# Hybrid attention and expert block on one core: three projections by feature tile, one gate slab moved into the last attention steps, statistics by quarters, and products of ones in three waits

## What is computed

```
h = layer_norm(concat(meta, x))
z = h @ w_in + b_in          # qa ka va | qb kb vb | forget gate | ga gb
oa = sliding_window_attention(qa, ka, va, sinks, rel_table)
ob = forgetting_attention(qb, kb, vb, cumsum(log_sigmoid(f)))
merged = sigmoid(ga) * (oa @ w_pa) + sigmoid(gb) * (ob @ w_pb)
h = layer_norm(ALPHA * h + merged @ w_o)
y = peer_ffn(h, ...)         # product keys, top 16, one-neuron experts
out = layer_norm(ALPHA * h + y)[16:]
```

## Time and profile before

| | |
|---|---|
| median of 3 executions | 1705.8 us (1704.66 to 1707.39) |
| the profiled execution's own time | 1718.5 us |
| its span | 1716.4 us |
| busy: PE, DVE, ACT, POOL | 1653.8, 1339.5, 735.2, 452.1 us |
| mean share of the DMA engines' rate | 255 GB/s |

### The profile page before, as it was taken

How to read it: one execution, slowest core, us unless ns; L and a number is a source line. 1 busy time by engine, 2 the same in 40 slices (tenths; PEclk the granted TensorE clock), 3 DMA queues, 4 the chain that set the end, 5 groups by cost and what they waited for, 6 DMA issues and landing times. The chain is left out here.

```text
span 1716.4 us, 26821 instructions
## 1 busy us (share of the span) xinstructions
PE 1653.8 (96%) x9808; PEld 1523.3 (89%) x9808; DVE 1339.5 (78%) x2848; ACT 735.2 (43%) x1288; POOL 452.1 (26%) x314
## 2 busy tenths in 40 slices
PE   5999999999979999999999999999999999999996
PEld 4897776577768899999999999999999999999996
DVE  5434554644467888999999989967989999999898
ACT  4214544333143354566766754434333333333331
POOL 0000000000001105133132432332544545457550
PEclk9999999889989999999999999999999999999998
DMA  5731111012214459699899999999999999999991
GB/s 167 198 95 55 39 48 38 25 49 86 74 61 155 129 157 379 217 341 336 269 316 340 353 307 332 341 398 392 382 400 410 407 408 408 407 402 409 407 404 78
DMA packets 185441, 438.47 MB, mean 255 GB/s; under 512 B 17832, under 2 KB 102000, under 8 KB 182880
## 3 DMA queue, kind: packets, MB, share of 16 engines
q1 hardware_dynamic: 73872, 227.43, 36.3%
q0 software_dynamic: 44080, 161.06, 25.5%
q10 hardware_dynamic: 67360, 48.28, 8.5%
HBM read 380.57 MB, written 56.13 MB: 254 GB/s over the span
## 5 line engine op out<-in xcount | busy, mean ns | idle before, releaser
L464 PE MATMUL psS<-hT_lo,hi 128*128 128x368 f32 (+2 forms) x1504 | 518.4, 345 | 4.6 <-DVE hT_lo L1021 3.9
L465 PE MATMUL psS<-hT_hi,lo 128*128 128x368 f32 (+2 forms) x1504 | 510.1, 339 | 0.0
L466 PE MATMUL psS<-hT_hi,hi 128*128 128x368 f32 (+2 forms) x1504 | 508.5, 338 | 0.0
L455 DVE TENSOR_TENSOR lo<-raw,hi 128x1024 fp32r<-128x1024 f32 x323 | 394.6, 1222 | 119.7 <-ACT hi L451 110.5
L451 ACT ACTIVATE hi<-raw 128x1024 fp32r<-128x1024 f32 x323 | 340.0, 1053 | 177.4 <-PE psS L466 124.0
L569 POOL DMA_INDIRECT gat<-in_u_rows,idx x144 | 214.7, 1491 | 393.1 <-DVE gat L1195 214.8
L464 PEld LDWEIGHTS psS<-hT_lo,hi 128*128 128x128 f32 x1504 | 283.8, 189 | 30.8 <-issue 15.6
L466 PEld LDWEIGHTS psS<-hT_hi,hi 128*128 128x128 f32 x1504 | 283.9, 189 | 13.4
L465 PEld LDWEIGHTS psS<-hT_hi,lo 128*128 128x128 f32 x1504 | 283.8, 189 | 11.1
L569 POOL DMA_INDIRECT gat<-in_v_exp,idx x144 | 220.8, 1533 | 233.9 <-DVE gat L1195 151.4
L766 ACT ACTIVATE act_hi<-act_t 128x368 fp32r<-128x368 f32 x128 | 65.6, 513 | 278.9 <-DVE act_t L1246 264.0
(11 more groups left out here) (303 smaller groups left out, 2630.1 us busy)
## 6 DMA issues: line engine op xcount, KB each, us to landing
raw<-in_u_exp SPq DMA_DIRECT2D x128, 512.0 KB
raw<-in_v_exp SPq DMA_DIRECT2D x128, 512.0 KB
gelu_dram<-gelu ACTq DMA_DIRECT2D x128, 184.0 KB
gates_dram<-gates ACTq DMA_DIRECT2D x92, 256.0 KB
gel_in<-gelu_dram SPq DMA_DIRECT2D x128, 184.0 KB
raw<-in_w_merge SPq DMA_DIRECT2D x24, 512.0 KB
gate_even<-gates_dram SPq DMA_DIRECT2D x8, 1472.0 KB
gate_odd<-gates_dram SPq DMA_DIRECT2D x8, 1472.0 KB
```

Source lines behind the costliest of these rows:

```text
L455: nc.vector.tensor_tensor(lo[:, n % RING, :], raw[:, n % RING, :], hi[:, n % RING, :].bitcast(F32), ALU.subtract).then_inc(lo_done, 1)
L464: nc.tensor.matmul(out_ap, w_h, x_l, start=start, stop=False)
L465: nc.tensor.matmul(out_ap, w_l, x_h, start=False, stop=False)
L466: return nc.tensor.matmul(out_ap, w_h, x_h, start=False, stop=stop)
```

## The change

1. Opening: DVE fills `ones` first, and PE multiplies `ones` by `ones` 52 times into bank 7; nobody reads the result. PE turns the first feature tile as soon as each token tile is normalised. DVE writes the low parts of slabs 0 to 2 ahead of all `hT_lo`. Slabs 0, 1 and 2 are then multiplied tile by tile, behind the turns of the next feature tile, into banks 4 to 7. The bias product and DVE's sum behind it (`w_done`) move behind slab 4 and slab 5.
2. Attention: `TILES` loses a tile in steps 14, 15, 32, 33, 36, 37 and two in step 38 and has 2 in each of steps 44 to 47. The 14th gate slab (v = 13) goes into bank 6 (`psO[:, 0, :]`), once the seventh block of heads is out of it. DVE's `oT_lo` comes one iteration later.
3. Merge: the gate slabs for m = 7 go ahead of all mix slabs, into both halves of `psS[:, 1]`; the weights are laid out in that order. The first slab of the output projection waits for one tile of `m_lo` at a time.
4. Statistics by quarters: two feature tiles of all token tiles share two banks (4 and 5, 6 and 7, 1 and 3, 4 and 5 again), read as four groups of 256.
5. Two more runs of products of ones, 36 behind the last turn and 30 behind the spread diagonals.

```diff
-FIRST_MIX = FIRST_MERGE + N_GATE
+FIRST_MIX = FIRST_MERGE + 2 * KT
...
-TILES = [4] * 16 + [2] * 16 + [3, 3, 2, 2, 2, 2, 2, 0] + [0] * 8
+TILES = [4] * 14 + [3] * 2 + [2] * 16 + [2, 2, 2, 2, 1, 1, 0, 0] + [0, 0, 0, 0, 2, 2, 2, 2]
...
+        def sum_bank(c, t):
+
+            return banks[((4, 5), (6, 7), (1, 3), (4, 5))[c][t // 2]]
...
+        def gate_bank(v):
+
+            return psS[:, v % 2, SEQ:] if v < N_GATE - 1 else psO[:, 0, :]
...
+            V.memset(ones[:, :], 1.0).then_inc(ones_set, 1)
...
+            for n in range(N_EARLY):
+                split_lo(dve, n)
             for k in range(KT):
                 dve.wait_ge(xT_done, k + 1)
                 dve.wait_ge(hT_hi_done, k + 1)
                 V.tensor_tensor(hT_lo[:, k, :], xT[:, k % 2, :], hT_hi[:, k, :].bitcast(F32),
                                 ALU.subtract).then_inc(hT_lo_done, 1)
-                if k < AHEAD:
-                    split_lo(dve, k)
-            V.memset(ones[:, :], 1.0).then_inc(ones_set, 1)
-
-            dve.wait_ge(bias_in, 64)
-            dve.wait_ge(w_mm, 1)
-            V.tensor_tensor(wrow[:, 0, :], psO[0:HEADS, 0, 0:3 * P], wrow[:, 1, :], ALU.add).then_inc(w_done, 1)
-            own.link(V.tensor_scalar(snk[:, 1, :], snk[:, 0, :], -1.0, None, ALU.mult))
...
-                w = block_ended(s - 3)
+                w = block_ended(s - 4)
...
-            def half_stats(c):
+            def quarter_stats(c):
 
                 dve.wait_ge(r_turned, c + 1)
                 for t in range(NBLK):
-                    ins = V.bn_stats(stats1[:, t, 6 * c:6 * c + 6], banks[4 + t])
+                    ins = V.bn_stats(stats1[:, t, 6 * c:6 * c + 6],
+                                     sum_bank(c, t)[:, t % 2 * (SEQ // 2):(t % 2 + 1) * (SEQ // 2)])
                     if t < NBLK - 1:
                         own.mark(ins)
                 ins.then_inc(r_stats_done, 1)
-                dve.wait_ge(r_stats_done, c + 1)
...
+                if m >= 3 and m % 2 == 1:
+                    quarter_stats((m - 3) // 2)
...
+            quarter_stats(3)
+            dve.wait_ge(r_stats_done, 4)
...
+            def keep_running(bank, times):
+
+                for _ in range(times):
+                    mm(bank[:, 0:P], ones[:, :], ones[:, :], start=True, stop=True)
+
             all_k = [(k, k) for k in range(KT)]
+            pe.wait_ge(ones_set, 1)
+            keep_running(banks[7], 52)
...
+            for k in range(KT + 1):
+                if k < KT:
+                    if k >= 2:
+                        pe.wait_ge(xT_done, k - 1)
+                    for t in range(NBLK):
+                        if k == 0:
+                            pe.wait_ge(norm_done, t + 2)
+                        turn(psS[:, k % 2, t * P:(t + 1) * P], xin[:, t, k * P:(k + 1) * P], ident)
+                    if k == 0:
+                        pe.wait_ge(norm_done, NBLK + 2)
+                    turn(psS[:, k % 2, SEQ:COLS], xin[0:META, NBLK, k * P:(k + 1) * P],
+                         ident[0:META, 0:META]).then_inc(turned, 1)
+                if k >= 1:
+                    j = k - 1
+                    if j == 0:
+                        pe.wait_ge(lo_done, N_EARLY)
+                    pe.wait_ge(hT_lo_done, k)
+                    for n in range(N_EARLY):
+                        halves = [slice(0, HALF), slice(HALF, COLS)] if n == 0 else [slice(0, SEQ)]
+                        for b, cols in enumerate(halves):
+                            out_ap = banks[4 + b][:, 0:HALF] if n == 0 else banks[5 + n]
+                            last = slab(n, n, out_ap, lambda k: hT_hi[:, k, cols], lambda k: hT_lo[:, k, cols],
+                                        [(j, j)], ends=(j == 0, j == KT - 1))
+                        if j == KT - 1:
+                            last.then_inc(slab_used, 1)
...
+                    mm(psO[0:HEADS, 0, 0:3 * P], relb[:, :], buck[:, :], start=True, stop=True).then_inc(w_mm, 1)
...
+                        if v == N_GATE - 1:
+                            pe.wait_ge(o_hi_done, 2 * NBLK - 1)
+                            pe.wait_ge(o_lo_done, 2 * NBLK - 1)
...
+                n = FIRST_MERGE + N_GATE + j
+                pe.wait_ge(lo_done, n + 1)
+                slab(n, n % RING, psS[:, 1, j * SEQ:(j + 1) * SEQ], tokens, tokens_lo, all_k).then_inc(slab_used, 1)
...
-                pe.wait_ge(m_lo_done, KT)
                 if m >= 2:
                     pe.wait_ge(r_done, m - 1)
-                slab(n, n % RING, psS[:, m % 2, 0:SEQ], lambda k: m_hi[:, k, :], lambda k: m_lo[:, k, :],
-                     all_k).then_inc(slab_used, 1)
+                for k in range(KT):
+                    if m == 0:
+                        pe.wait_ge(m_lo_done, k + 1)
+                    last = slab(n, n % RING, psS[:, m % 2, 0:SEQ], lambda k: m_hi[:, k, :], lambda k: m_lo[:, k, :],
+                                [(k, k)], ends=(k == 0, k == KT - 1))
+                last.then_inc(slab_used, 1)
...
+            pe.wait_ge(r_stats_done, 2)
+            keep_running(banks[7], 36)
             for part, (done, bank) in enumerate(((diag_done, 1), (shift_done, 3))):
                 pe.wait_ge(done, NBLK)
                 for t in range(NBLK):
                     last = mm(banks[bank][:, t * P:(t + 1) * P], ones[:, :], diag[:, part * NBLK + t, :],
                               start=True, stop=True)
                 last.then_inc(spread_done, 1)
+            keep_running(banks[7], 30)
```

More of the change, by code:

```diff
@@ L640, in _ @@
                                          ACT.Copy).then_inc(o_hi_done, 1)
+            for j in range(2):
+                split_hi(act, FIRST_MERGE + N_GATE + j + AHEAD)
             for m in range(KT):
@@ L644, in _ @@
                     act.wait_ge(mix_done, m - 1)
-                if m < KT - 1:
-                    split_hi(act, FIRST_MIX + m + AHEAD)
-                    for j in range(2):
+                split_hi(act, FIRST_MIX + m + AHEAD)
+                for j in range(2):
+                    if m < KT - 1:
                         nc.scalar.activation(gate[:, m % 2, j, :], gate_input(2 * m + j), ACT.Sigmoid).then_inc(gate_done, 1)
[L649 to L656, removed]
+                    else:
+                        act.wait_ge(slab_used, FIRST_MERGE + N_GATE + j + 1)
+                        nc.scalar.activation(gate[:, m % 2, j, :], psS[:, 1, j * SEQ:(j + 1) * SEQ], ACT.Sigmoid,
+                                             bias=bcol[:, N_PROJ + 8 * j + m:N_PROJ + 8 * j + m + 1]).then_inc(gate_done, 1)
                 act.wait_ge(mix_done, m + 1)
@@ L860, in halves @@
                     return v.rearrange("p (b c) -> p b c", b=2)
-                ps = halves(psS[:, n % 2, :])[:, :, 0:HALF]
+                whole = psT[:, :] if n == 0 else psS[:, n % 2, :]
+                square = banks[5 + n] if 1 <= n < N_EARLY else psS[:, n % 2, 0:SEQ]
+                ps = halves(whole)[:, :, 0:HALF]
                 if n == 0:
@@ L897, in _ @@
             dve.wait_ge(ck_in, 16)
-            for s in range(N_STEPS + 4):
+            for s in range(N_STEPS + 5):
                 last_step = 1 <= s <= N_STEPS
@@ L961, in _ @@
                                     oT_hi[:, w // NBLK, :, cols].bitcast(F32), ALU.subtract).then_inc(o_lo_done, 1)
+            for j in range(2):
+                split_lo(dve, FIRST_MERGE + N_GATE + j + AHEAD)
             for m in range(KT):
-                last = FIRST_MIX + m if m < KT - 1 else FIRST_OUT - 1
-                for n in range(FIRST_MIX + m, last + 1):
-                    split_lo(dve, n + AHEAD)
-                dve.wait_ge(slab_used, last + 1)
+                split_lo(dve, FIRST_MIX + m + AHEAD)
+                dve.wait_ge(slab_used, FIRST_MIX + m + 1)
                 dve.wait_ge(gate_done, 2 * m + 2)
@@ L1362, in _ @@
-            pe.wait_ge(bias_in, 64)
-            mm(psO[0:HEADS, 0, 0:3 * P], relb[:, :], buck[:, :], start=True, stop=True).then_inc(w_mm, 1)
+            for k in range(KT + 1):
[23 more added lines that the diff above has]
+                            last.then_inc(slab_used, 1)
@@ L1374, in _ @@
                         half = slice(b * HALF, (b + 1) * HALF)
-                        if n == 0 and b == 0:
-                            for k in range(KT):
-                                pe.wait_ge(hT_lo_done, k + 1)
-                                slab(n, 0, psS[:, 0, 0:HALF], lambda k: hT_hi[:, k, half], lambda k: hT_lo[:, k, half],
-                                     [(k, k)], ends=(k == 0, k == KT - 1))
-                            continue
                         last = slab(n, n % RING, psS[:, n % 2, b * SEQ:b * SEQ + HALF], lambda k: hT_hi[:, k, half],
```

69 lines of the change are left out of this document (32 added, 37 removed).

## The result

| | before | after |
|---|---|---|
| median | 1705.6 us (4 executions, 1704.7 to 1707.4) | 1687.3 us (4 executions, 1686.0 to 1691.1) |
| span of the profiled execution | 1716.4 us | 1686.2 us |
| busy: PE, DVE, ACT, POOL | 1653.8, 1339.5, 735.2, 452.1 us | 1659.7, 1341.2, 733.8, 449.3 us |

The ratio is 0.9895, with a 95% interval from 0.9876 to 0.9914: about 1% faster, inside the range given, but by 18.3 us and not by the 30.2 forecast. From profiled execution to profiled execution the gain is 30.2 us (1716.4 to 1686.2), so the two ways of measuring disagree by 12 us. The kernel before has two groups of execution times. Of the 69 taken in all of this study's comparisons, 44 lie between 1704.1 and 1711.2 (median 1706.7) and 25 between 1715.8 and 1724.7 (median 1717.6). The profiled execution, 1718.5, is of the upper group; the three behind the median of 1705.8 are of the lower one.

What follows compares the result with a forecast made beforehand. TensorE, working 1653.8 of 1716.4 us, was taken as the bound, with gains only in the first 510 us. The terms 3.5 + 15.5 + 6.4 + 5.8 - 1.0 = 30.2 us, off 1705.8, gave 1675.6 us; range 1667 to 1689.

Steps and rivals of the forecast that it cites:

- the median is 12.7 lower, and nothing in the terms depends on that part: Summing step: terms read from the 1718.5 us profiled execution were taken unchanged off the 1705.8 us median.
- (a): Rival, attention steps 38 to 43: the clock falls and returns with the fillers, 10.8 us lost, 1686.4 us; chance 0.14.
- What bounds the kernel: Whole program: TensorE is busy 1653.8 of 1716.4 us; gain only in the first 510 us, from idle time and low clock.
- Opening: Start to slab 3: first slab product at 21.5 us, cold start assumed, slab 3 4.1 us earlier; 3.5 us gained.
- Attention: Attention steps to the merge: waits for probabilities go and later steps take 3.2 us at full clock; 15.5 us gained.
- Merge to output: Merge and output projection: the 3.59 us wait for `m_lo` and 2.8 us of low clock go; 6.4 us gained.
- Statistics: Statistics after the output projection: the 3.34 us stop goes, with 2.5 us more behind it; 5.8 us gained.
- Last two waits: Last turn to query stage's end: products of ones outlast the waits, ending at 32.5 us against 31.5; 1.0 us lost.
- (d): Rival, attention: clock falls as in (a) and stays low from step 38 to the merge; 35.3 us lost, 1710.9; chance 0.03.
- (b): Rival, opening: turns between products keep the clock low until slab 3; 17.5 us more, 1693.1 us; chance 0.06.
- (c): Rival: clock holds through the opening and PE leaves the last two waits earlier; 2.9 + 2 us more, 1670.7; chance 0.13.

Runs made afterwards that it cites:

- e2: The changed kernel with the attention part undone (fillers, bank and `oT_lo` as before): 1700.7 us, ratio 0.9927 against the kernel before.
- e7: The kernel before with one edit, `oT_lo` one softmax iteration later, which takes out the stops for probabilities: 1702.4 us, ratio 0.9946.
- e1: The kernel before again, no edit, against itself: 1707.0 us, ratio 0.9974.
- e3: The changed kernel with the first output slab waiting for all eight tiles of `m_lo` again: 1693.8 us, ratio 0.9901 against the kernel before.
- e11: The changed kernel with the statistics in halves again and the 36 products of ones in bank 3: 1692.7 us, ratio 0.9890 against the kernel before.
- e5: The changed kernel again, no edit: 1686.9 us, ratio 0.9856 against the kernel before.
- e10: The changed kernel with 15 more products of ones ahead of the first slab product: 1686.3 us, ratio 0.9851 against the kernel before.
- e6: The changed kernel with 23 and 18 products of ones for 36 and 30 in the last waits, and 15 more in the opening: 1682.1 us, ratio 0.9825.
- e9: The changed kernel with the old filler table and the 14th gate slab's old bank and waits, `oT_lo` still one iteration later: 1688.5 us, ratio 0.9860.
- e8: The changed kernel with 23 and 18 products of ones for 36 and 30 in the last two waits: 1685.9 us, ratio 0.9846.

## Why the prediction was right, and where it was wrong

**The step that failed** is "the median is 12.7 lower, and nothing in the terms depends on that part". The attention term does. The low clock of 329.8 to 355.5 us, on which it rests, is what makes an execution of the upper group: e2's profile holds the clock behind the same stop, e7, without the stop, has no upper group, and the upper group's granted clock over the span is lower by 0.0076 (e1). The medians of the two groups are 10.9 us apart. Against executions of the lower group attention is therefore worth 15.5 less 10.9, 4.6 us, and e7 measured 4.3. With that the sum is 30.2 less 10.9, 19.3 us, and 1705.8 less 19.3 is 1686.5; measured were 1687.3 and 1686.9. I had the warning in hand: a profiled execution 12.7 us above three others is a fact about the profile, and a sum of terms read from it can't be taken off their median before that difference has a place.

That the median still fell inside the range is luck: 1687.3 is 11.7 us above the forecast, and the range reached up to 1689 mainly to take in rival (a), a fall of the clock in the changed kernel, which didn't happen.

The same holds, smaller, for the clock behind the two later stops. The profile of before had its low stretch behind each; e1, e7, e3 and e11 show the same stops followed by 0.75 or 0.52 in the one place and 0.70 or 1.00 in the other. Nor do the parts add up in medians: taken back one at a time from the change they cost 13.8 (e2), 6.9 (e3) and 5.8 us (e11), with 2 to 3 for the opening more than the 18.3 of the whole, since most executions of e2 pay for the clock and most of the kernel before don't.

Point by point, from profile to profile:

- **What bounds the kernel**: right. From the query stage's end the rest is 1205.3 us for 1206.1.
- **Opening, 3.5 forecast, 2.0 measured** (the first scores of attention, 146.64 to 144.62). Slab 3 was to be 4.1 earlier and is 3.0 (48.95 to 45.96); behind it the bias product and what goes with it take back 1.0 where 0.6 was counted. First slab product at 21.29 for 21.5, a cold start there as assumed. A tile with its turns took 2.9 us (the sets of turns start at 28.98 and then every 2.9 us up to 40.61) for the 2.70 that I took; that is the mis-sized term. The change's second profile, e5, has slab 3 at 44.89, so this start varies by 1 us, and the gain is 3.1 there. With 15 more ones (e10, e6) slab 3 is 5.6 and 5.4 us earlier (43.37 and 43.55) and the first scores 4.6 and 4.4, against a bound of 6.4.
- **Attention, 15.5 forecast.** The first product of the output projection starts 22.0 us earlier (398.84 for 420.86). Of that 3.6 is the stop for `m_lo` and 2.0 was there when the stage began (its first scores 144.62 for 146.64), which leaves 16.4; the steps without fillers take the assumed 3.2 us. The size was right in the profile. Of the fillers the prediction gained 5.6 us ahead of 316.64 and gave 5.6 back behind it, so it had their move at nothing, and e9 bears that out: 0.2 us in the trace (1.6 in medians). All of the term stood on the two stops and the clock.
- **Merge to output, 6.4**: 6.9 in medians, 5.3 in the trace (e3). **Statistics, 5.8**: 5.8 in medians, 3.6 in the trace (e11). From profile to profile of before and after the two are 12.5 (3.6, and 57.9 for 49.0 from the first output product to the last turn) for 12.2. Both stops are gone, and the clock is 1.00 behind both places; the stops are the certain part, the low clock behind them the part that varies.
- **Last two waits, 1.0 lost**: 1.5 lost, 33.0 us for 31.5 from the last turn's end. A product of ones took 0.223 and 0.221 and not 0.213 (8.04 us by 36, 6.62 by 30), and that small loss is all of the difference. It was seen that the ones outlast what they cover; that they could be cut was not followed up, and e8 and e6 show 4.6 us there (28.4 and 28.5 for 33.0).

**The rivals.** (a) and (d), a fall of the clock in steps 38 to 43: not seen; the window from 306.6 has 1.00, and e7 and e9 ran eight steps without fillers at 1.00. (b), turns between the products keep the clock low: refuted. Turns between slab products take 0.60 us for four from 28.98 on, at 1.00, and 1.05 only in the cold stretch at 25.30; so the strong reading of the Trainium skill's rule ("TensorE: Matmul & The Clock Gate", Part 4) doesn't hold where products are most of the work. (c), the clock holds through the opening: not in the change, but with 15 more ones it holds at the first slab product. The median lies by (a)'s 1686.4 by accident: none of its mechanism is there. The isolated gap of 56 ns that the same page of the Trainium skill gives for a product of 128 columns, section "Back-to-back issue gap", doesn't describe these float32 products: 0.223 us each here, four times that.

## What to carry to other kernels

Before a sum of terms is taken off a median, compare the profiled execution's own time with the others: where they differ by more than their spread, find which term holds the difference, since a stop may cost its own length in one execution and its length plus a spell of low clock in the next. When a stop is found, ask first which single instruction stands in the waited-for engine's way; here one line of DVE's order was worth about 4 us in the kernel before where the clock held and 15 in the third of the executions where it fell, and a table of fillers next to nothing. One profile per kernel can't price the clock behind a stop: look at several, or at the granted clock of every execution. Products that nobody reads pay only if they end with the wait: count them by their measured duration, and cut them to it.

## What the runs showed of the hardware

- The same stop of 1.8 us, in the same place of the same order, was followed by a granted clock of 0.52 to 0.54 for some 25 us (before, e1) or by 1.00 (e2). In 69 executions of the kernel before, 25 were in the longer group; in e2, 9 of 12 were.
- The stop of 3.34 us for the statistics was followed by 0.50 (before), 0.70 (e1) or 1.00 (e7, e11) over some 5.5 us; the stop of 3.59 us for `m_lo` by 0.51 (before), 0.52 (e7), 0.75 (e1) or 0.74 (e3) over 6.3 us.
- The stop of 1.23 us left the clock at 1.00 in e1 (at 302.96) and before, and was followed by 0.54 from 303 to 306 us in e2 (at 300.24). Idle times of 0.46 us left it alone in e7 and e9. The 3.14 us in the opening of the profile after were followed by 0.50 from 21.3 to 27.0 us.
- The clock column is not always the clock. In the profile of before it reads 1.00 from 0 to 34.5 us, yet four turns take 1.09 to 1.11 us there, as in the stretch at 0.50 and not as in those at 1.00 (0.60), and products of 264 columns follow each other in 0.22 us until 34.34 and in 0.12 from then on. In a program's first tens of us, durations have to be read in its place.
- From an idle start the first ten products of ones took 4.3 us, 0.43 each (1.0 to 5.3 us in the profile after, where the column reads 1.00); the 36 in the last waits took 0.223 each.
